# One recurrence of a two-layer trunk: the order of a chunk's steps on VectorE, TensorE, GpSimd and the DMA queue changed

## What is computed

```
def step(state, inp):
    r_t, w_t, k_t, v_t, kk_t, a_t = inp
    sk = einsum('bhij,bhj->bhi', state, kk_t)
    state = state * w_t - sk (x) (kk_t * a_t) + v_t (x) k_t
    y = einsum('bhij,bhj->bhi', state, r_t)
...
y = (y - mean) * rsqrt(var + GN_EPS) * ln_w + ln_b
bonus = sum(r * k * r_k, axis=-1) * v
y = (y + bonus) * g
```

## Time and profile before

| | |
|---|---|
| median of 3 runs | 3098.84 us (3096.55 to 3102.23) |
| profiled execution | time 3100.76 us, span 3098.8 us |
| busy, share of the span | PE 87%, DVE 53%, POOL 41%, ACT 30% |
| granted PE clock, mean | 0.944 of full |
| recurrence | about 1626 to 2236 us of the span |

### The profile page before, as it was taken

The page is one execution under the profiler, slowest core; times in us unless marked ns, Lnnn a source line. Parts: engine busy times, 40 slices in busy tenths (PEclk is TensorE's granted clock), DMA queues, the critical chain, the costliest instruction groups (busy, mean ns, idle before and its releaser), DMA issues. The chain is left out here.

```text
span 3098.8 us, 48344 instructions
## 1 busy us (share of the span) xinstructions
PE 2688.0 (87%) x20064; PEld 2195.1 (71%) x20064; DVE 1655.4 (53%) x2070; ACT 932.7 (30%) x1543; POOL 1257.8 (41%) x630
## 2 busy tenths in 40 slices
PE   1787898999999999899994777777569999999999
PEld 1565666888877788677773667666557888878887
DVE  6844545756536444669734666776314544434444
ACT  2434433222233222455542223222124222222221
POOL 2532244444454444443433234333136344444443
PEclk9889998999999999999996888888789999999999
DMA  6421233555523223375563333333243233323333
GB/s 233 165 73 35 89 121 113 170 168 170 170 84 106 89 88 103 95 171 154 144 157 89 90 84 86 81 88 76 47 112 89 95 95 95 102 89 95 102 96 122
DMA packets 313433, 343.31 MB, mean 111 GB/s; under 512 B 231041, under 2 KB 231169, under 8 KB 313217
## 3 DMA queue, kind: packets, MB, share of 16 engines
q1 hardware_dynamic: 313216, 340.23, 37.5%
HBM read 298.29 MB, written 40.89 MB: 109 GB/s over the span
## 5 line engine op out<-in xcount | busy, mean ns | idle before, releaser
L687 POOL TENSOR_TENSOR wl<-w,wh 128x1024 fp32r<-128x1024 f32 x368 | 907.4, 2472 | 1304.0 <-ACT wh L728 1303.9
L180 PE MATMUL ps<-hi,wh 128*128 128x512 f32 x2208 | 881.8, 399 | 56.6 <-POOL wl L687 42.9
L181 PE MATMUL ps<-lo,wh 128*128 128x512 f32 x2208 | 868.3, 393 | 0.0
L182 PE MATMUL ps<-hi,wl 128*128 128x512 f32 x2208 | 867.9, 393 | 0.0
L728 ACT ACTIVATE wh<-w 128x1024 fp32r<-128x1024 f32 x368 | 388.1, 1056 | 716.2 <-DMA w<-in_ffn_w_in 528.7
L180 PEld LDWEIGHTS ps<-hi,wh 128*128 128x128 f32 x2208 | 419.8, 190 | 159.5 <-POOL wl L687 43.1
L994 DVE SCALAR_TENSOR_TENSOR xt<-ps,mod,xt 128x512 f32<-128x512 f32 x384 | 286.5, 750 | 431.8 <-PE ps L182 431.5
L181 PEld LDWEIGHTS ps<-lo,wh 128*128 128x128 f32 x2208 | 419.8, 190 | 89.3 <-issue 3.5
L182 PEld LDWEIGHTS ps<-hi,wl 128*128 128x128 f32 x2208 | 419.3, 190 | 89.6
L999 DVE TENSOR_TENSOR act<-ps,silu 128x512 f32<-128x512 f32 x88 | 60.9, 692 | 456.3 <-PE ps L182 456.3
L180 PE MATMUL ps<-act_hi,wh 128*128 128x512 f32 x704 | 281.7, 400 | 17.3 <-DVE act_lo L1003 9.7
(11 more groups left out here) (219 smaller groups left out, 3403.9 us busy)
## 6 DMA issues: line engine op xcount, KB each, us to landing
w<-in_ffn_w_in SPq DMA_DIRECT2D x176, 512.0 KB, 3.7
piece<-in_ada_w SPq DMA_DIRECT2D x96, 512.0 KB, 4.7
w<-in_ffn_w_out SPq DMA_DIRECT2D x88, 512.0 KB, 3.7
w<-in_w_rkv SPq DMA_DIRECT2D x48, 512.0 KB, 4.1
scratch<-silu SPq DMA_DIRECT2D x48, 256.0 KB, 3.1
scratch<-act SPq DMA_DIRECT2D x48, 256.0 KB, 3.0
w<-in_wqk SPq DMA_DIRECT2D x20, 512.0 KB, 4.7
xt<-in_xT SPq DMA_DIRECT2D x4, 2048.0 KB, 10.3
```

The costliest lines, as they stand in the source:

```text
L180: pe.matmul(out, w_hi(k), x_hi(k), start=first and k == 0, stop=False)
L181: pe.matmul(out, w_hi(k), x_lo(k), start=False, stop=False)
L182: ins = pe.matmul(out, w_lo(k), x_hi(k), start=False, stop=last and k == kc - 1)
L687: pool.tensor_tensor(wl[n % NW][:, :, :], wr[n % NW][:, :, :], wh[n % NW][:, :, :].bitcast(F32), ALU.subtract).then_inc(*wlo.up)
```

## The change

The steps by_feature, affine, finish and store_z of a solved chunk move to the period after the one in which it is solved, as a sixth stage zp; on PE by_feature stands behind solve_x. Period 21 is added for chunk 15. begin moves ahead of the inversion on DVE, bonus_value ahead of scale. norms waits for bonus_value of the chunk before. r is loaded by itself (`load_r`), the other three tiles ahead of blocks_out, as soon as POOL is through with them. POOL's bonus_terms waits for r and for b_dec; keys begins with lprev. bias has two buffers. The gate is loaded a period later. ACT does squares ahead of the last token_out.

```diff
-                    for c in range(-RING, NC + 1):
-                        period(at(c + 3), at(c + 2), at(c + 1), at(c), at(c - 1))
+                    for c in range(-RING, NC + 2):
+                        period(at(c + 3), at(c + 2), at(c + 1), at(c), at(c - 1), at(c - 2))
...
                         def load_tiles(ch):
 
+                            sp.wait_ge(*g["k2_done"].at(ch))
+                            sp.wait_ge(*g["lq_done"].at(ch))
+                            sp.wait_ge(*g["b_done"].at(ch))
+                            settle(sp)
+                            for n, x in ((1, kt_), (4, at_), (3, st_)):
...
+                        def load_r(ch):
                             sp.wait_ge(*g["rk_done"].at(ch))
                             sp.wait_ge(*g["ar_done"].at(2 * ch))
                             settle(sp)
-                            for n, x in ((0, rt), (1, kt_), (3, st_), (4, at_)):
...
-                        def period(w, x, d, y, zz):
-                            if y is not None:
-                                load_gate(y)
+                        def period(w, x, d, y, zz, zp):
+                            if zz is not None:
+                                load_gate(zz)
+                            if w is not None:
+                                load_tiles(w)
                             if x is not None:
                                 blocks_out(x)
                             if w is not None:
-                                load_tiles(w)
+                                load_r(w)
                             if x is not None:
                                 blocks_in(x)
+                            if zp is not None:
+                                store_z(zp)
                             if d is not None:
                                 blocks_back(d)
                             if w is not None:
                                 load_values(w)
-                            if zz is not None:
-                                store_z(zz)
...
                         def keys(ch):
 
+                            pool.wait_ge(*g["l_done"].at(ch + 1))
+                            pool.tensor_tensor(lprev[:, :, :], lcum[:, :, :], st_[:, :, :], ALU.subtract).then_inc(*g["lq_done"].up)
                             pool.wait_ge(*g["t1_done"].at(ch + 1))
...
                         def bonus_terms(ch):
                             pool.wait_ge(*g["k2_done"].at(ch + 1))
+                            pool.wait_ge(*g["r_in"].at(ch + 1))
+                            pool.wait_ge(*g["bb_done"].at(ch + 1))
...
-                            if x is not None:
-                                normed_keys(x)
                             if zz is not None:
                                 bonus_and_bias(zz)
                             if x is not None:
-                                bonus_terms(x)
-                            if zz is not None:
-                                finish(zz)
+                                normed_keys(x), bonus_terms(x)
+                            if zp is not None:
+                                finish(zp)
                             if w is not None:
                                 keys(w)
...
+                            if w is not None:
+                                squares(w)
                             if x is not None:
                                 token_out(x, 1)
-                            if w is not None:
-                                squares(w)
...
                         def norms(ch):
                             pe.wait_ge(*g["sq_done_w"].at(ch + 1))
-                            pe.wait_ge(*g["z1_done"].at(max(ch - 3, 0)))
+                            pe.wait_ge(*g["bonus_done"].at(ch))
...
                         def by_feature(ch):
                             pe.wait_ge(*g["ybd_done"].at(ch + 1))
                             pe.wait_ge(*g["bonus_done"].at(min(ch + 4, NC)))
+                            pe.wait_ge(*g["mx_done"].at(min(ch + 5, NC)))
...
                             if zz is not None:
                                 solve_x(zz)
+                            if zp is not None:
+                                by_feature(zp)
...
-                                by_token(x, 0), by_token(x, 1), bonus_sums(x), gram(x, 1)
-                            if zz is not None:
-                                by_feature(zz)
-                            if x is not None:
-                                by_token(x, 2)
+                                by_token(x, 0), by_token(x, 1), bonus_sums(x), gram(x, 1), by_token(x, 2)
...
                         def begin(ch):
-                            dve.wait_ge(*g["tiles_in"].at(4 * ch + 4))
+                            dve.wait_ge(*g["tiles_in"].at(3 * ch + 3))
                             dve.wait_ge(*g["kb_done"].at(ch))
+                            dve.wait_ge(*g["rk_done"].at(ch))
...
                             if x is not None:
                                 bounded(x)
+                            if zp is not None:
+                                affine(zp)
...
                             if x is not None:
                                 decayed_keys(x)
+                            if w is not None:
+                                begin(w)
                             if d is not None:
                                 invert(d)
                             if zz is not None:
                                 variance(zz)
                             if d is not None:
                                 invert_last(d)
+                            if x is not None:
+                                bonus_value(x)
                             if zz is not None:
                                 scale(zz)
-                            if x is not None:
-                                bonus_value(x)
-                            if w is not None:
-                                begin(w)
-                            if zz is not None:
-                                affine(zz)
                             if w is not None:
                                 decay_sums(w)
```

More of the change, by code:

```diff
@@ L94 @@
 wkv_ybd_done wkv_yf_done wkv_z1_done wkv_bias_done wkv_z_step wkv_zeros g_in0*16 g_in1*16
-wkv_chunk_used wkv_post_done wkv_sub_step wkv_sub_done n_out*16 nd_in*16 t_out*16 img_zero*16 t_in0*16 t_in1*16 z_stored*16 z_in0*16 z_in1*16 z_hi z_lo stored*16
+wkv_chunk_used wkv_post_done wkv_r_in*16 wkv_sub_step wkv_sub_done n_out*16 nd_in*16 t_out*16 img_zero*16 t_in0*16 t_in1*16 z_stored*16 z_in0*16 z_in1*16 z_hi z_lo stored*16
 w_in0*16 w_in1*16 w_in2*16 w_in3*16 whi wlo tile_done x_done silu_done act_mul act_hi act_done
@@ L1248, in wkv_phase @@
                 state, xst, ust = st("state"), st("x_st"), st("u_st")
-                yc, ysq, yn, z, bias = st("y_centred"), st("y_sq"), st("y_norm"), st("z"), st("bias")
+                yc, ysq, yn, z, bias = st("y_centred"), st("y_sq"), st("y_norm"), st("z"), [st(f"bias{b}") for b in range(2)]
                 mean, var = sb("mean", [P, PAIRS], c=c), sb("var", [P, PAIRS], c=c)
@@ L1258, in wkv_phase @@
                          "m_step yc_done ysq_done var_done yrt_done yrn_done ybd_done yf_done z1_done bias_done z_step "
-                         "zeros sub_step sub_done chunk_used post_done").split()
-                g = {n: sig("wkv_" + n, 16 if n in ("tiles_in", "v_in") else 1) for n in names}
+                         "zeros sub_step sub_done chunk_used post_done r_in").split()
+                g = {n: sig("wkv_" + n, 16 if n in ("tiles_in", "v_in", "r_in") else 1) for n in names}
                 g_in = [sig(f"g_in{b}", 16) for b in range(2)]
@@ L1321, in load_tiles @@
                         def load_tiles(ch):
+                            sp.wait_ge(*g["k2_done"].at(ch))
[3 more added lines that the diff above has]
+                            for n, x in ((1, kt_), (4, at_), (3, st_)):
+                                sp.dma_start(x[:, :, :], scr[n, bass.ds(ch, 1)].rearrange("c p a n -> (c p) a n")).then_inc(*g["tiles_in"].up)
+                        def load_r(ch):
                             sp.wait_ge(*g["rk_done"].at(ch))
@@ L1325, in load_tiles @@
                             settle(sp)
-                            for n, x in ((0, rt), (1, kt_), (3, st_), (4, at_)):
-                                sp.dma_start(x[:, :, :], scr[n, bass.ds(ch, 1)].rearrange("c p a n -> (c p) a n")).then_inc(*g["tiles_in"].up)
+                            sp.dma_start(rt[:, :, :], scr[0, bass.ds(ch, 1)].rearrange("c p a n -> (c p) a n")).then_inc(*g["r_in"].up)
                         def load_values(ch):
@@ L1405, in keys @@
                             pool.tensor_tensor(k2[:, :, :], k2[:, :, :], kt_[:, :, :], ALU.add).then_inc(*g["k2_done"].up)
-                            pool.wait_ge(*g["l_done"].at(ch + 1))
-                            pool.tensor_tensor(lprev[:, :, :], lcum[:, :, :], st_[:, :, :], ALU.subtract).then_inc(*g["lq_done"].up)
```

(5 more changed lines are left out.)

## The result

The changed kernel took 3105.53 us (median of 20 runs, 3097.82 to 3111.47) against 3100.34 us for the kernel before (20 runs): ratio 1.0018, interval 1.0011 to 1.0025. Forecast were 3092.1 us and a range of 3075 to 3101. The mean of the four is 1.0000. So the changed order is worth nothing that can be measured, where a gain of 6.75 us was forecast.

A forecast was written before the change was run, and what follows sets the result against it. Bound: a hand-over chain into level_x, the blocks' return only about 0.7 us shorter, then the level chain and mostly DVE work. Periods -1.1, filling -2.8, draining -2.85 sum to -6.75: from 3098.84 to 3092.1 us, range 3075 to 3101.

The forecast's parts named there:

- T to L: From T, the end of DVE's inversion, to L, PE's start of level_x; forecast 9.80 us, 10.46 before.
- L to D: From PE's start of level_x to D, DVE's start of ar; forecast 7.12 us, 5.92 before.
- D to T: From DVE's start of ar to the end of the next inversion; forecast 17.12 us, 17.65 before.
- the draining: Last chunks: solve_x of chunk 15 no longer waits behind by_feature of chunk 14; -2.85 us.
- (a): Ahead of level_x: the inverted blocks' return through memory, 9.8 us after the inversion, sets its start; gain 0.66 us.
- (b): PE idles 2 to 3.5 us ahead of level_x and the clock drops; costs 1.2 us, bounds 0 and 2.4.
- (c): POOL's rk waits for b_dec, so DVE's ar no longer runs beside it; 1.73 us won.
- (d): begin's kk and k on DVE move ahead of the inversion, where nothing covers them; +1.2 us.
- (e): Filling and draining of the recurrence: -2.8 us at the start, -2.85 us at the end.
- The clock stays full: Rival, 20%: by_feature keeps PE busy enough ahead of level_x to hold the clock; -21.1 us, 3078 us.
- No measurable gain: Rival, 17%: slower blocks' return or half the periods paying 2.4 us; total 0 to -3, 3096 to 3099 us.
- Slower: Rival, 8%: low clock from level_x through solve_u in every period; +7.5 us, 3106 us.

The follow-up runs named there:

- Experiment 1: Changed kernel with the four block loads issued before the inversion ends, fetching an older chunk's blocks, so level_x doesn't wait for its own: 3025.81 us, ratio 0.9775.
- 13: Changed kernel with the v and gate loads held until the inverted blocks are back: 3090.68 us, ratio 0.9978.
- 4: Changed kernel with unused filler matmuls on PE, 6 ahead of norms and 8 behind by_feature: 3089.23 us, ratio 0.9973.
- 3: Changed kernel with begin put back behind bonus_value: 3066.72 us, ratio 0.9902.
- 2: Kernel before with one added line, POOL's rk waiting for b_dec: 3074.16 us, ratio 0.9928.
- 8: Changed kernel without the wait of POOL's rk on b_dec: 3098.58 us, ratio 1.0006.
- 11: Second series of the changed kernel with begin put back behind bonus_value: 3066.36 us, ratio 0.9889.
- 9: Changed kernel with begin back behind bonus_value and the v and gate loads held until the inverted blocks are back: 3058.70 us, ratio 0.9861.
- 10: Changed kernel with begin back behind bonus_value, v and gate loads held, two of four block loads on ACT's queue: 3060.37 us, ratio 0.9874.

## Why the prediction was wrong

Its mechanism for T to L and L to D was right, and so were these two legs, within 0.1 us. Two terms of its sum failed: D to T with begin in it, and the draining at the end. The sum was made of small differences near zero, and these two terms are 5.5 of its 6.75 us (2.9 and 2.55). The mean of two or four profiles goes by "before" and "after" here.

**(a) The second path into L: right.** T + 9.8 was forecast, 9.81 measured. Experiment 1 shows that it sets L. The gate load that "may slow the blocks' return by some tenths" was not in the 9.8; 13 measures 0.67 for gate and v together, and how much of it is the gate was not tested. So some of the close agreement may be luck.

**(b) The price of arriving early: right in size, put down to the wrong part.** L to D was forecast as 7.12 and is 7.05; 4 takes 0.93 of it back. The Trainium skill (TensorE: Matmul & The Clock Gate, HAM oscillation) has bursts with a DMA wait between them cold every time, in a case with waits of 3 to 5 us; here, with holes of 1.4 to 4.4 us, 36 of 48 periods were cold and 12 not. The working gave the price to by_feature's move. 3 shows that it hangs on begin: with by_feature moved and begin late, 18 of 24 periods keep 5.92 or 5.93.

**(c) rk: right in size and in the collision, wrong in what ends it.** 1.73 forecast, 1.70 in the period shown, 1.63 in 2. In the old order the added wait is enough by itself (2); in the new one ar keeps 0.69 without it (8). The Trainium skill (SBUF — State Buffer, Who interferes with whom) has a port pair that DVE and GpSimd share under an exclusive lock; ar at 1.58 beside rk and 0.69 without agrees.

**(d) begin ahead of the inversion: the first step that failed.** "D to T: 17.65 - 1.73 + 1.2 = 17.12" is 17.27. In the period shown n_t to T grew by 1.34 and not 1.2: k_dec to kk takes 0.77 where other neighbours stand 0.60 apart. With begin late, most periods of 3 have a D to T of 15.90, where the changed kernel's have 17.29: begin costs 1.39 there. And "less 1.2 for the last" is 0.67 (its D to T is 16.62 instead of 17.29), since there DVE's operation on the state takes 1.39 beside POOL. Over the twelve periods D to T is 207.2 us, where 12 x 17.12 - 1.2 = 204.2 was forecast: 2.9 more. L to D gives 0.9 back. The twelve periods were forecast at -1.1 and are +1.4 (409.45, before 408.07).

**(e) The edges: the draining is the second.** Filling was forecast at -2.8 and gave -4.0, from the start of the recurrence to the T that begins the twelve periods (120.4, before 124.4). Draining was forecast at -2.85 and gave -0.3 (from the T that ends them to the last z: 68.8, before 69.0), though single profiles lie far apart: 67.0 to 71.4, before 67.3 and 70.7. What was named did happen: in the first pair of profiles it is 11.8 us from the state of chunk 14 to that of chunk 15 (2216.36 to 2228.13), and was 14.7. The time ahead of it grew. In that pair T to L of chunk 15 is 9.8, where it was 8.7, and PE stands 7.14 us ahead of it, where it stood 2.92. Over all profiles T to L of chunk 15 is 9.0 to 9.8, before 8.6 and 8.7, and the last T to the last z is shorter by only 1.2 (37.9, before 39.1 in both). The period ahead of that T is longer by 0.9 (30.8, before 29.9), which is less than the two profiles of before differ in it (28.2 and 31.6). The forecast had applied the return and the clock to the full periods alone.

**Sum.** +1.4 - 4.0 - 0.3 = -2.9 us within the recurrence, where -6.75 was forecast. Outside it, in code that is the same, the profiles of the changed kernel are longer by about 3: the front is 1625.2 to 1628.7 us (1625.2 and 1625.8 before), the part behind 869.3 to 873.0 (869.3 twice). In the first pair of profiles the front alone differs by 3.0. Why it varies stays open, and with four profiles against two it may be chance. Open is also how much of the first series' 5.2 us is such variation. The range ended at 3101 because it took its upper end from a period of 34.6 and no account of this.

**The rivals.** "The clock stays full" is out: 4 had to keep PE busy for it. "No measurable gain" is what happened over four series, but not in its way: its period was 34.4 to 34.6 and the measured one is 34.12; the edges and D to T made the difference. "Slower" had L to D at 8.3 everywhere; it was over 8 in 7 of 48 periods. No rival had begin as the part that decides: by 3 and 11 it alone costs about 1% (0.9902 and 0.9889 without its move, 1.0000 with it), though the working had both halves of that price, 1.2 in D to T and a hole of 2 to 3.5 us.

## What to carry to other kernels

Ahead of a wait for a transfer, making an engine early buys nothing and can cost its clock; give it there the work that has to be done anyway (here begin's 1.2 us on DVE, which kept norms and PE back), and look for what lengthens the transfer. Change one step at a time: of this edit one part was worth 0.7%, another minus 1%, and the whole showed neither. Where the forecast is a difference of legs near zero, give the no-change case most of the chance, and apply each effect to the filling and draining periods too.

## What the runs showed of the hardware

- Two loads of a 128x512 tile, issued 0.1 and 0.8 us behind the last of four small block loads, lengthened T to L by 0.6 to 0.7 us (9 and 11, 13 and 15), though all four had been issued ahead of them. Splitting the four over two queues gave nothing (9 and 10: 3058.70 and 3060.37).
- The price of a hole on PE ahead of L grew with it, on average. Over the thirteen profiles of kernels with the new order and the blocks' return in it, 54 periods with no hole or one up to 1.5 us had a mean L to D of 5.95; the 28 with more than 3 us had 7.56, at most 8.40, but two of them stayed at 5.93. The 74 between had 6.69, 29 of them without any price. The chain from L to D is mostly matmuls, with DVE's additions and ACT's copies between, so most of what the low clock adds to them shows in L to D.
- Beside POOL's two products rk even a DVE operation on 128x8 (the scaling of the mean) took about 0.41 us in most periods of the changed kernel and once 0.85 in experiment 3, against 0.17 throughout the kernel before, where rk was through.
